# Two-part fp32r products in the feed-forward layers: one 512-column matmul for hi and lo operand

## The reference

```python
def swiglu(x, w_in, w_out):                       # four times; w_in 1024 x 5632, w_out 2816 x 1024
    gate, up = jnp.split(x @ w_in, 2, axis=-1)
    return (jax.nn.silu(gate) * up) @ w_out
...
h = layer_norm(DN_ALPHA * h + 0.5 * swiglu(h, ffn_w_in[i, 0], ffn_w_out[i, 0]), ln_g[i, 0], ln_b[i, 0])
...
h = jnp.square(jax.nn.relu(jnp.einsum('bsd,df->bsf', x, w_ff1[layer])))     # once; w_ff1 1024 x 4096
y = jnp.einsum('bsf,fd->bsd', h, w_ff2[layer])
x = _layer_norm(DEEPNORM_ALPHA * x + y, ln2_g[layer], ln2_b[layer])
```

## Time and profile before

| what | value |
|---|---|
| median of 3 runs | 1587.61 us (1587.33 to 1589.15) |
| the profiled execution, its own time | 1587.47 us |
| its span in the trace | 1585.7 us |
| mean granted clock of TensorE | 0.999 |
| PE busy | 1561.2 us, 9892 matmuls |
| DVE busy | 897.2 us |
| ACT busy | 699.4 us |
| DMA | 283.94 MB, 179 GB/s on the mean |

### The profile page before, as it was taken

How to read it: one execution, slowest core, us unless ns; L and a number is a source line. 1 busy time by engine, 2 the same in 40 slices (tenths; PEclk the granted TensorE clock), 3 DMA queues, 4 the chain that set the end, 5 groups by cost and what they waited for, 6 DMA issues and landing times.

```text
span 1585.7 us, 23577 instructions
## 1 busy us (share of the span) xinstructions
PE 1561.2 (98%) x9892; PEld 1393.9 (88%) x9892; DVE 897.2 (57%) x855; ACT 699.4 (44%) x617; POOL 126.4 (8%) x149
## 2 busy tenths in 40 slices
PE   8999999999999999999999999999999999999998
PEld 7999988789998999989878799998999788889997
DVE  5445566564545644565457654447585456775555
ACT  5343355344334433443334443434436556453442
POOL 1000011110001000012221100001003200010000
PEclk9999999999999999999999999999999999999999
DMA  7555454255554555556444455555444235455551
GB/s 298 186 187 186 186 193 179 106 186 186 186 186 159 213 188 187 185 194 229 167 161 158 166 220 184 181 193 214 159 158 175 105 135 184 152 196 187 187 187 76
DMA packets 41727, 283.94 MB, mean 179 GB/s; under 512 B 4912, under 2 KB 5232, under 8 KB 8752
## 3 DMA queue, kind: packets, MB, share of 16 engines
q1 hardware_dynamic: 37728, 270.55, 47.1%
q0 software_dynamic: 2368, 8.59, 1.6%
q10 hardware_dynamic: 1552, 3.64, 0.6%
HBM read 281.65 MB, written 1.05 MB: 178 GB/s over the span
## 4 chain that ended last, share of the span: by engine, by line
PE 93%; DVE 3%; ACT 2%; POOL 2%; issue 1%; DMA 0%; DVEq 0%; POOLq 0%; ACTq 0%
PE psum L1365 29%; PE psum L1368 29%; PE psum L1369 29%; PE psum L1377 1%; ACT squares L429 1%; PE psum L1639 1%; DVE normalised L868 1%; POOL att_p L381 1%; POOL ln_rstd L292 0%; DVE normalised L837 0%; DVE weights_lo L807 0%; PE psum L1728 0%; PE psum L1782 0%; POOL ln_rstd L291 0%; PE psum L1750 0%
## 5 line engine op out<-in xcount | busy, mean ns | idle before, releaser
L807 DVE TENSOR_TENSOR weights_lo<-weights_raw,weights_hi 128x2048 fp32r<-128x2048 f32 x249 | 574.0, 2306 | 461.2 <-ACT weights_hi L408 459.4
L408 ACT ACTIVATE weights_hi<-weights_raw 128x2048 fp32r<-128x2048 f32 (+1 forms) x256 | 485.1, 1895 | 438.4 <-PE psum L1369 429.6
L1365 PE MATMUL psum<-operand_hi,weights_hi 128*128 128x256 f32 x1952 | 553.7, 284 | 0.0
L1368 PE MATMUL psum<-operand_lo,weights_hi 128*128 128x256 f32 x1952 | 552.4, 283 | 0.0
L1369 PE MATMUL psum<-operand_hi,weights_lo 128*128 128x256 f32 x1952 | 552.4, 283 | 0.0
L1365 PEld LDWEIGHTS psum<-operand_hi,weights_hi 128*128 128x128 f32 x1952 | 374.5, 192 | 4.3 <-issue 2.2
L1368 PEld LDWEIGHTS psum<-operand_lo,weights_hi 128*128 128x128 f32 x1952 | 374.5, 192 | 1.8
L1369 PEld LDWEIGHTS psum<-operand_hi,weights_lo 128*128 128x128 f32 x1952 | 374.5, 192 | 0.0
L1365 PE MATMUL psum<-weights_hi,operand_hi 128*128 128x512 f32 x512 | 205.4, 401 | 6.1 <-DVE weights_lo L850 4.8
L1368 PE MATMUL psum<-weights_lo,operand_hi 128*128 128x512 f32 x512 | 200.7, 392 | 0.0
L1365 PE MATMUL psum<-weights_hi,hidden_hi 128*128 128x512 f32 x480 | 188.1, 392 | 0.2
(11 more groups left out here) (248 smaller groups left out, 1084.6 us busy)
## 6 DMA issues: line engine op xcount, KB each, us to landing
weights_raw<-in_weights SPq DMA_DIRECT2D x256, 1024.0 KB, 4.8
ln_rows<-in_ln_rows POOLq DMA_DIRECT2D x16, 512.0 KB, 4.8
normalised<-in_x SPq DMA_DIRECT2D x2, 512.0 KB, 6.3
ret_constants<-in_ret_constants ACTq DMA_DIRECT2D x1, 1024.0 KB, 4.8
out<-normalised SPq DMA_DIRECT2D x4, 256.0 KB, 2.0
att_constants<-in_att_constants ACTq DMA_DIRECT2D x1, 576.0 KB, 4.6
gla_w_low<-in_gla_w_low ACTq DMA_DIRECT2D x1, 512.0 KB, 3.3
att_w_small<-in_att_w_small ACTq DMA_DIRECT2D x1, 512.0 KB, 3.6
```

Source lines behind the costliest of these rows:

```text
L408: nc.scalar.activation(w_hi[:, s, whole], raw[:, s, whole], ACT.Copy).then_inc(hi_split, 1)
L807: nc.vector.tensor_tensor(w_lo[:, s, :], raw[:, s, :], w_hi[:, s, :].bitcast(F32), ALU.subtract).then_inc(lo_split, 1)
L1365: mm(out, a_hi, b_hi, start=start, stop=False, skip_group_check=True)
L1368: mm(out, a_hi, b_lo, start=False, stop=False, skip_group_check=True)
```

## The change

`x_hi` and `x_lo` become two interleaved halves of one tile, `x_both[:, c, 0 or 1, :]`, so that 512 consecutive columns hold a chunk of the hi and of the lo operand. In units 3 to 10 of the four gated layers and in units 2 to 7 of the last one, `features_both` takes the place of `features_unit`: for each chunk and block, one matmul of 512 columns with the hi weights (hi·hi into the first half of a bank, hi·lo into the second) and one of 256 columns with the lo weights (lo·hi into the first half). A block of 128 features then has a bank to itself, and a unit takes all four banks of `work`. To put the two halves of each bank together, ACT copies the second halves (`against_lo`) into a new tile `gate_up`, DVE adds the first halves (`against_hi`) to it, and the activation reads `gate_up`. In the gated layers ACT's order becomes: two splits, two copies (gate, up), the third split, silu, `hidden_hi`; DVE's: two splits, two additions, the third split, `hidden`, `hidden_lo`. In the last layer ACT makes one copy of 1024 columns, DVE one addition and one combined max-and-multiply. PE waits for `up_summed` in place of `hid_done` before the next features (in the last layer still for `hid_done`). The copies of the operand tiles elsewhere get the new strides.

```diff
@@ -83,8 +83,8 @@
-        x_hi = sb("operand_hi", [P, KC, TOK], F32R)
-        x_lo = sb("operand_lo", [P, KC, TOK], F32R)
+        x_both = sb("operand", [P, KC, 2, TOK], F32R)
+        x_hi, x_lo = x_both[:, :, 0, :], x_both[:, :, 1, :]
...
@@ -100,6 +100,7 @@
+            gate_up = sb("gate_up", [P, 4, TOK], F32, ph)
...
@@ -189,6 +190,7 @@
+        against_lo_copied, gate_summed, up_summed = sem("against_lo_copied"), sem("gate_summed"), sem("up_summed")
...
@@ -223,6 +225,8 @@
+        against_hi, against_lo = work[:, :, 0:TOK], work[:, :, TOK:2 * TOK]
+        summed_before = lambda f, j: (FFN_STEPS - 3) * f + j - 3
...
@@ -411,8 +415,7 @@
-                    nc.scalar.activation(hi[:, 2 * b:2 * b + 2, :].rearrange("p c t -> p (c t)"), work[:, (b + swap) % 4, :],
-                                         ACT.Copy).then_inc(turned_hi, 1)
+                    nc.scalar.activation(hi[:, 2 * b:2 * b + 2, :], two(work[:, (b + swap) % 4, :]), ACT.Copy).then_inc(turned_hi, 1)
...
@@ -468,13 +471,27 @@
+                def summed_step(j, i=0):
+
+                    ahead = n0 + 3 * j + 1
+                    split_hi(ahead - 1, 3 * i)
+                    split_hi(ahead, 3 * i)
+                    act.wait_ge(weights_used, i * 9 + n0 + 3 * j)
+                    for half in (slice(0, 2), slice(2, 4)):
+                        nc.scalar.activation(gate_up[:, half, :], against_lo[:, half, :], ACT.Copy).then_inc(against_lo_copied, 1)
+                    split_hi(ahead + 1, 3 * i)
+                    act.wait_ge(gate_summed, i * 3 + summed_before(f, j) + 1)
+                    nc.scalar.activation(silu_g[:, :, :], gate_up[:, 0:2, :], ACT.Silu).then_inc(silu_done, 1)
+                    act.wait_ge(hid_done, i * 3 + j0 + j + 1)
+                    hidden_hi(j0 + j, j % 3, hid[:, 0:2, :], i)
+
                 step(1, n0 + 2, n0 + 5, pairs[1])
                 step(2, n0 + 4, n0 + 7, pairs[0])
                 for j in range(3, 5):
-                    step(j, n0 + 3 * j - 2, n0 + 3 * j + 1, pairs[1])
+                    summed_step(j)
                 with act.Fori(0, 2) as i:
                     for j in range(5, 8):
-                        step(j, n0 + 3 * j - 2, n0 + 3 * j + 1, pairs[1], i)
+                        summed_step(j, i)
...
@@ -767,8 +783,12 @@
                     split_hi(n, 4 * i)
                 split_hi(n + 1, 4 * i)
-                act.wait_ge(hid_ready, i * 3 + j0 + s)
-                relu_up(n - 2, pairs[0], i)
+                if s == 1:
+                    act.wait_ge(hid_ready, j0 + 1)
+                    relu_up(n - 2, pairs[0])
+                else:
+                    act.wait_ge(weights_used, i * 12 + n)
+                    nc.scalar.activation(gate_up[:, :, :], against_lo, ACT.Copy).then_inc(against_lo_copied, 1)
...
@@ -811,8 +831,8 @@
-                    pair = lambda t: t[:, 2 * b:2 * b + 2, :].rearrange("p c t -> p (c t)")
-                    nc.vector.tensor_tensor(pair(lo), work[:, (b + swap) % 4, :], pair(hi).bitcast(F32),
+                    pair = lambda t: t[:, 2 * b:2 * b + 2, :]
+                    nc.vector.tensor_tensor(pair(lo), two(work[:, (b + swap) % 4, :]), pair(hi).bitcast(F32),
...
@@ -904,13 +924,30 @@
+                def summed_step(j, i=0):
+
+                    ahead = n0 + 3 * j + 1
+                    split_lo(ahead - 1, 3 * i)
+                    split_lo(ahead, 3 * i)
+                    dve.wait_ge(against_lo_copied, i * 6 + 2 * summed_before(f, j) + 1)
+                    nc.vector.tensor_tensor(gate_up[:, 0:2, :], against_hi[:, 0:2, :], gate_up[:, 0:2, :],
+                                            ALU.add).then_inc(gate_summed, 1)
+                    dve.wait_ge(against_lo_copied, i * 6 + 2 * summed_before(f, j) + 2)
+                    nc.vector.tensor_tensor(gate_up[:, 2:4, :], against_hi[:, 2:4, :], gate_up[:, 2:4, :],
+                                            ALU.add).then_inc(up_summed, 1)
+                    split_lo(ahead + 1, 3 * i)
+                    dve.wait_ge(hid_ready, i * 3 + j0 + j)
+                    dve.wait_ge(up_summed, i * 3 + summed_before(f, j) + 1)
+                    hidden(j0 + j, gate_up[:, 2:4, :], i)
+                    hidden_lo(j0 + j, j % 3, hid[:, 0:2, :], i)
+
                 step(1, n0 + 5, pairs[1])
                 step(2, n0 + 7, pairs[0])
                 for j in range(3, 5):
-                    step(j, n0 + 3 * j + 1, pairs[1])
+                    summed_step(j)
                 with dve.Fori(0, 2) as i:
                     for j in range(5, 8):
-                        step(j, n0 + 3 * j + 1, pairs[1], i)
+                        summed_step(j, i)
...
@@ -1328,6 +1364,16 @@
+            def summed_square(n, s, i=0):
+
+                dve.wait_ge(against_lo_copied, i * 3 + 2 * summed_before(4, 3) + s - 1)
+                summed = nc.vector.tensor_tensor(gate_up[:, :, :], against_hi, gate_up[:, :, :], ALU.add)
+                summed.then_inc(up_summed, 1)
+                dve.wait_ge(up_summed, i * 3 + summed_before(4, 3) + s - 1)
+                dve.wait_ge(hid_ready, i * 3 + j0 + s)
+                nc.vector.scalar_tensor_tensor(out=hid[:, :, :], in0=gate_up[:, :, :], scalar=0.0, in1=gate_up[:, :, :],
+                                               op0=ALU.max, op1=ALU.mult).then_inc(hid_done, 1)
+
...
@@ -1338,7 +1384,10 @@
                 split_lo(n + 1, 4 * i)
-                square(j0 + s, pairs[0], i)
+                if s == 1:
+                    square(j0 + 1, pairs[0])
+                else:
+                    summed_square(n, s, i)
...
@@ -1432,6 +1481,21 @@
+                    last.then_inc(weights_used, 1)
+
+            def features_both(n, i=0):
+
+                for s in range(2):
+                    slot = slot_of(n + s)
+                    pe.wait_ge(lo_split, i + (n + s + 1))
+                    for k in range(4):
+                        c = 4 * s + k
+                        for b in range(4):
+                            cols = slice(k * NCOL + b * P, k * NCOL + (b + 1) * P)
+                            mm(work[:, b, :], w_hi[:, slot, cols], x_both[:, c, :, :].rearrange("p a t -> p (a t)"),
+                               start=c == 0, stop=False, skip_group_check=True)
+                            last = mm(against_hi[:, b, :], w_lo[:, slot, cols], x_hi[:, c, :],
+                                      start=False, stop=c == KC - 1, skip_group_check=True)
...
@@ -1504,8 +1568,11 @@
                     at = 2 * (j % 3)
                     down(n0 + 3 * j + 6, hid_hi, hid_lo, range(at, at + 2), j == 0, False, 9 * i)
-                    pe.wait_ge(hid_done, i * 3 + j0 + j + 3)
-                    features_unit(n0 + 3 * j + 7, pairs[1], i=9 * i)
+                    if j == 0:
+                        pe.wait_ge(hid_done, j0 + 3)
+                    else:
+                        pe.wait_ge(up_summed, i * 3 + summed_before(f, j + 3))
+                    features_both(n0 + 3 * j + 7, i=9 * i)
...
@@ -1918,7 +1985,10 @@
                     pe.wait_ge(hid_done, i * 3 + j0 + s)
-                features_unit(n, pairs[0], i=12 * i, between={4: lambda: turn_hidden(j0, 4 * P)} if s == 1 else {})
+                if s == 1:
+                    features_unit(n, pairs[0], between={4: lambda: turn_hidden(j0, 4 * P)})
+                else:
+                    features_both(n, i=12 * i)
```

More of the change, by code:

```diff
@@ L579, in quarter_hi @@
                     act.wait_ge(turned, turns["ret"] + 2 * h + b + 1)
-                    nc.scalar.activation(ret_hi(4 * h + 2 * b).rearrange("p c t -> p (c t)"), quarter_pair[h][:, b, :],
-                                         ACT.Copy).then_inc(turned_hi, 1)
+                    nc.scalar.activation(ret_hi(4 * h + 2 * b), two(quarter_pair[h][:, b, :]), ACT.Copy).then_inc(turned_hi, 1)
             for u in range(8, 12):
@@ L1081, in quarter_lo @@
                     dve.wait_ge(turned_hi, turns["ret"] + 2 * h + b + 1)
-                    flat = lambda t: t.rearrange("p c t -> p (c t)")
-                    nc.vector.tensor_tensor(flat(r_lo[:, c:c + 2, :]), quarter_pair[h][:, b, :],
-                                            flat(ret_hi(c)).bitcast(F32), ALU.subtract).then_inc(operand_ready, 1)
+                    nc.vector.tensor_tensor(r_lo[:, c:c + 2, :], two(quarter_pair[h][:, b, :]), ret_hi(c).bitcast(F32),
+                                            ALU.subtract).then_inc(operand_ready, 1)
             split_lo(n - 5)
```

## The result

The changed kernel takes 1590.87 us (median of 16 runs, 1589.17 to 1593.96) against 1587.40 us (1587.16 to 1589.24): a ratio of 1.0021, 95% interval 1.0014 to 1.0029. It is slower by a fifth of a percent, where 1579.2 us and a gain of 0.5% were forecast. The profiled execution is the slowest of the 16, 1593.96 us at a mean granted clock of 0.995; eight of the others have 0.997, and the fastest 0.998.

The account below looks back on a forecast made before the run. The prediction took PE to bound the kernel: 1587.47 - 15.8 us (merges) + 7.4 us (last units) = 1579.1, shown as a median of 1579.2 us, 0.53% faster. Its own range was 1577.5 to 1582.5; the 8-in-10 range 1575 to 1587.

Parts of the forecast that it names:

- What bounds the kernel: Feed-forward loops: bound by PE, number of matmuls times start distance; other engines have about half their time to give.
- Part 1: Feature matmuls in 38 units: 1216 merges save 13 ns each, 15.8 us in all.
- only the first held: Bound on merge saving: if only the longer 512-column starts behind 256 held, 6 ns a merge, 7.3 us in all.
- in a change there and back they cancel: Matmul length changes: up to 7 ns more going to 512 and 7 ns less going back cancel, leaving 13 ns.
- Part 2: ACT's copies and DVE's additions in the loops: hidden under PE, nothing charged; DVE 9.5 and ACT 8 us a pass.
- Part 3: Last unit of each gated layer: `hidden_lo` later, PE's third tile starts 1.86 us later, 7.4 us lost over four layers.
- Part 4: Interleaved operand layout: strided writes, contiguous reads; costed at nothing, 10% on each copy would be 2 us.
- The first: Rival in `features_both`: a merge saves less; 1587.6 us at 6 ns, 1595.0 at 0 ns; chance 0.12, 0.05 in slower part.
- the loops waited: Rival in the loops: features wait until the four banks are summed; 0.5 us a unit gives 1598 us; chance 0.04.
- the tail hidden: Rival at gated layers' ends: last unit's delay disappears behind the norm or splits reorder, 1571.8 us; chance 0.05.
- The signs of being wrong: Three signs: a pair over 354 ns, a PE wait for `up_summed`, or the gap at the gated layer's end missing.

Follow-up runs that it names:

- copies without the merge: Changed kernel with the old 256-column matmuls but all its copies, second DVE passes and their order; five runs, 1594.93 to 1602.92 us, ratio 1.0085.
- four and four: Changed kernel with the four merged matmuls of each chunk first, then its four of 256 columns; 1586.84 us, ratio 0.9995.
- sixteen and sixteen: Changed kernel with the 16 merged matmuls of each weight tile first, then its 16 of 256 columns; 1584.92 us, ratio 0.9977.
- nothing of 256 columns: Changed kernel with the lo-weight matmul also taking all 512 columns, adding lo times lo to the second half; 1712.5 us in a single run.
- late and early silu: Late: kernel before with third split ahead of silu and multiplication in units 3 to 10, 1590.82 us. Early: changed kernel with both ahead of that split, 1586.03 us.

## Why the prediction was wrong, point by point

- **What bounds the kernel.** Right: PE, with no wait in the loops, before and after.
- **Part 1, 13 ns a merge: the step that failed in size.** The term of 15.8 us measured 7.2 us (0.19 us a pass). The change gives 6 ns a merge, the lower bound of that part, though not by its reading of "only the first held": in the alternation a 512-column distance is 9 ns longer than 227 and a 256-column one 3 ns shorter than 120, and the bound looked at only the first two distances behind a change of length. The reasoning "in a change there and back they cancel" was wrong: a pass before holds one change there and back among 120 matmuls, so its sum couldn't show a cost of some 20 ns, 0.1% of it. The starts to the nanosecond do show it: behind a stretch of 256 columns the next five distances of 512 are 233, 236, 228, 233 and 231 ns and only then about 227, so that every merged matmul of an alternation stands in that region. Sixteen in a row bring the 13 ns back, and without 256-column neighbours the dearness is gone. What in PE causes it stays open. Nor is it the 2.5 ns a merge of the rule cited in the prediction (the Trainium skill, "TensorE: Matmul & The Clock Gate", section "Back-to-back issue gap", which gives it for a matmul by itself): three orders measured 6, 9 and 13 ns.
- **Part 2, the loops.** Right: DVE 9.46 and ACT 7.77 us a pass (forecast 9.5 and 8), no wait for `up_summed`, and copies without the merge leave the pass as it was. DVE's busy time rose by 48.2 us, where the prediction has some 51 (its own terms add up to 52.0).
- **Part 3, the last unit.** Right in mechanism and size: 7.4 us forecast, 7.46 measured by the copies without the merge, 7.5 in the list of waits.
- **The step that was left out: the clock behind the wait.** The prediction charged a wait of 1.9 us with 1.9 us. Behind three of the four such waits of the profiled run, TensorE's granted clock fell to 1.2 GHz for 3.4 us, at 1.6 us a time. In the median run this is worth some 3.2 us, and it is what makes the kernel slower rather than equal: without a fall it would stand at 1587.8 by the account above.
- **Part 4, the layout.** Right, 0.1 us.
- **The rivals.** The first came true in its milder half (6 ns a merge, 1587.6 us); the whole rival had a chance of 0.12, that half 0.07. It alone would have been a tie. Neither the loops waited, nor was the tail hidden.
- **The signs of being wrong.** None of the three that the prediction ends with showed: a pair takes 353 ns and not over 354, PE has no wait for `up_summed`, and the gap at the end is there. A limit of 354 ns let more than half of the gain go unnoticed, and no sign looked at the clock. What did show it was the pass, 16.79 us and not 16.56.

With the two misses in place the sum reads 1587.47 - 7.2 + 7.5 + 3.2 = 1591.0, measured 1590.87.

## What to carry to other kernels

Fewer and longer matmuls gain only their fixed cost, here 13 ns each, and all of it only where like stands beside like (strictly alternating, 6 ns): put the 512-column ones of a tile in a row and the short ones after them. An edit that is free in every pass of a loop must be worked out once more for the last pass, where the consumer comes early; one unit left in its old form was worth 9.7 us here. And a new idle stretch of PE is priced with what the clock does behind it: look at the mean clock of several runs, and at whether the run times stand in steps, not at the page's row of tenths alone.

## What the runs showed that was not expected

- Five matmuls of 512 columns behind a stretch of 256-column ones start 228 to 236 ns apart, the following ones about 227; alternating, a pair takes 353 ns, four and four 351, sixteen and sixteen about 347.
- The granted clock: 1.2 GHz for 3.4 us soon behind 1.88 and 1.89 us of idle PE (from 189.9, 504.0 and 695.1 us in the changed kernel), but not behind the fourth, which ends at 1085.94 us. It isn't certain: of the 20 such waits of 1.88 to 1.95 us in five profiled runs, 8 were followed by a fall (3 of 4 in the changed kernel, 2 each in four and four and in nothing of 256 columns, 1 in sixteen and sixteen, none in the copies without the merge). Of the 8 waits of 1.0 and 1.4 us in late and early silu none was. Kernels with waits of 1.0 or 1.4 us at the same places show no spread beyond that of the kernel before.
- A fall can also come behind work that counts as busy: in 3 of 12 traces soon behind the 2.05 us of 16 short matmuls on 8 rows in the attention layer.
- Run times stand on a ladder of about 1.6 us: 1587.3 and 1588.9 for the kernel before, 1594.9, 1599.6 and 1602.9 for the copies without the merge.
